# Second feed-forward block: its up product as seven half-size products per pair of weight blocks

## The chip, the cores and the metric

One core of a Trainium2 chip runs the program. The metric is the device time of one execution in microseconds (us). Engines are written as the profile writes them: PE is TensorE (matmuls; PEld its weight loads), ACT is ScalarE, DVE is VectorE, POOL is GpSimd, SP is SyncE, which issues the DMAs of the weights.

## The reference

A block of a network on 512 tokens (plus 256 context tokens) of width 1024: a feed-forward sublayer, a mixer (delta rule and attention), and a second feed-forward sublayer. The last one is what the change touches, on the 512 tokens alone:

```python
def _ffn_sublayer(x, shift, scale, gate, pre_g, post_g, w_gu, w_down):
    h = _modulate(_rmsnorm(x, pre_g), shift, scale)
    a, b = jnp.split(h @ w_gu, 2, axis=-1)
    y = (jax.nn.silu(a) * b) @ w_down
    return x + FFN_RES_WEIGHT * gate * _rmsnorm(y, post_g)
```

`w_gu` is 1024 x 5632 and `w_down` 2816 x 1024, in float32. All is computed to nearly float32 accuracy.

## The kernel before

Activations lie with the features on the 128 partitions: h is 8 tiles of 128 features by 512 tokens. A float32 product is made of three passes: each operand is split in a rounded part (`_hi`) and the rest (`_lo`), and `hi*hi + lo*hi + hi*lo` is accumulated in PSUM. A weight block is 128 outputs by 1024 inputs (8 slices of 128, 512 KB). Its way is the same everywhere: SP loads it to one of four slots of `raw` (`load`: it waits until `w_split` says that the slot's old block has been split); ACT rounds it to `w_hi` (`split`, L776); DVE subtracts to make `w_lo` (L1475) and raises `w_split`; PE uses it (`gemm`, L2283).

The second feed-forward block has 22 pairs of up blocks: one block of a pair is for `a` (its 128 columns), the other for `b`. ACT reads `a` out of PSUM through silu (`sg`), DVE multiplies with `b` (`gt`), ACT rounds (`g2_hi`), DVE subtracts (`g2_lo`). The 22 pairs are cut in chunks of 8, 8 and 6, and after each chunk comes a down product of 8 blocks (16 half blocks after the last: `last_down`), so that only 8 hidden tiles are held. Here a block is 8 slices x 3 passes = 24 matmuls of 512 columns.

The first two pairs are special (`first_up`): their matmuls are 256 columns wide, since the tokens' second half is still being normalised (`h_tile` on ACT, `n_scale` and `h_low` on DVE) when PE starts on the first.

The first feed-forward block of the same kernel already runs 20 of its 22 pairs in another way, as seven products of half size (a Winograd form of Strassen's scheme). A pair of blocks and the tokens are seen as a 2 x 2 matrix each: the weights' quarters are 4 slices of one block, the tokens' quarters 4 slices by half the tokens. Seven products of such quarters or of sums of them (A11, A12, S2, S3, S1, A22, S4) give the four quarters of the result where the plain way takes eight. POOL makes the four sums of weights of a pair (`weight_sums`, L641 to L648), ACT and DVE split all seven, two places of PSUM are added up by ACT and DVE. There a product is 12 matmuls of 384 columns.

Order of work is written out by hand on every engine; engines are in-order and wait on semaphores (`u_hi` and `u_lo`: how many quarters are rounded and split; `u_mm`: how many products are done; `w_loaded0..3`: a slot of `raw` is loaded; `w_split`: blocks split; `s_add`: weight sums made).

Of the kernel before, what the change touches and what calls it, by code (L numbers as in the profile page):

```python
# [23 lines left out]
P = 128  # L24
# [99 lines left out]
SLOTS = product_slot(N_SEVEN - 1, S4) + 1  # L124

# [52 lines left out]
def build(nc, W, WMOD, XT, VEC, CONV, CA, CB, OUT, XS, GR):  # L178
    ctx = ExitStack()
    with ctx:  # L180
# [140 lines left out]
        f_lo = at("f_lo", 148, [KT, SEQ], F32R)  # L321
        z_t = at("z_t", 87.5, [4, HALF])
# [146 lines left out]

        def token_sum(i):  # L470
# [295 lines left out]


        @block.scalar
        def _(a):
# [173 lines left out]
            def h_tile(h, k):  # L943
                n = KT * h + k
                a.wait_ge(s("nrm_ready"), 4 * KT + n + 1)
                if n >= 4:
                    a.wait_ge(s("h_ready"), 4 * KT + n - 3)
                a.activation(z_u[:, k % 4], z_t[:, k % 4], ACT.Identity, bias=mod[:, 48 + k, 1:2], scale=drv[:, 4, k, 1:2])\
                 .then_inc(s("h_full"), 1)
                a.wait_ge(s("h_full"), 4 * KT + n + 1)  # L950
                a.activation(f_hi[:, k, xhalf(h)], z_u[:, k % 4], ACT.Copy).then_inc(s("h_rounded"), 1)
# [125 lines left out]
            def ffn(i, b0, seg_list):  # L1077
                lo = seg_list[0][0]
                for kind, b, n, c, hid in ffn_parts(b0):
                    if kind == "down" and c == 2:  # L1080
# [3 lines left out]

                    def up(it):
                        first = i and c == 0 and isinstance(it, int)
                        for j in range(4):
                            blk = Blk(b, it, j)
                            if not first:
                                step(blk)  # L1090
                            elif j < 2:
                                a.wait_ge(s("gemm_done"), blk.n + 1)
                                split(blk.ahead(4))
                            if first and j == 2:
                                a.wait_ge(s("gemm_done"), blk.n + 1)
                                a.activation(sg[:, CTX:T], first_bank(blk, j), ACT.Silu).then_inc(psum_read[blk.pair], 1)
                            elif j % 2 == 0:
                                read_out(blk, lambda l, h_: sg[:, l:h_], seg_list, ACT.Silu)
                            else:

                                a.wait_ge(psum_read[blk.pair], blk.turn + 2)
                                p_ = it * 2 + j // 2
                                a.activation(cols(g_hi, g2_hi, i, bass.ds(p_, 1), lo, T), gt[:, lo:T], ACT.Copy).then_inc(s("g_rounded"), 1)

                    def down(it):
                        for j in range(4):
                            blk = Blk(b, it, j)
                            step(blk)
                            if c == 0:
                                read_out(blk, lambda l, h_: cols(Y, Y2, i, bass.ds(it * 4 + j, 1), l, h_), seg_list)  # L1110
                    if i and kind == "up" and c == 0:
                        up(0)
                        with a.Fori(1, n // 4, 1) as it:
                            up(it)
                    else:
                        loop(a, n // 4, up if kind == "up" else down)
# [343 lines left out]
            for k in range(KT):  # L1460
                x_square(1, k)
            x_rstd(1)
            for k in range(KT):
                h_tile(1, k)
            a.preload_act_table_set(SILU_SET)
            ffn(1, B_FFN2, segs_x)
# [3 lines left out]
        def _(v):  # L1470
# [145 lines left out]
            def h_low(h, k):  # L1616
# [5 lines left out]
                v.tensor_tensor(f_lo[:, k, xhalf(h)], z_u[:, k % 4], f_hi[:, k, xhalf(h)].bitcast(F32), ALU.subtract).then_inc(s("h_ready"), 1)  # L1622
# [135 lines left out]
            def ffn(i, b0, seg_list):  # L1758
                lo = seg_list[0][0]
                pairs = i * HID  # L1760
                for kind, b, n, c, hid in ffn_parts(b0):
                    if kind == "down" and c == 2:
                        all_read(v, b - 2 * FCH[c])
# [1252 lines left out]
```

## Time and profile before

| | |
|---|---|
| median of 3 runs | 1921.43 us (1920.65 to 1922.58) |
| the profiled execution | 1924.11 us, its span 1922.4 us |
| granted TensorE clock, mean | 0.996 |
| PE busy | 1873.6 us, 97% of the span |
| DVE busy | 1167.9 us, 61% |
| ACT busy | 893.4 us, 46% |
| POOL busy | 412.7 us, 21% |
| last part of the program | from 1569 us on: second feed-forward block past its first two pairs |

The span is the time from the first to the last instruction; the execution's own time is 1.7 us longer. The 40 slices of the page show the granted clock at nine tenths or more in each. In the last third of the span POOL has nothing to do.

### The profile page before, as it was taken

The page shows a single profiled execution, that of the slowest core. Times are in us where ns is not written, and L with a number is a line of the kernel's source. Part 1 is how long each engine was busy: PE and PEld are TensorE (multiplying, and loading weights), DVE is VectorE, ACT ScalarE, POOL GpSimd, SP SyncE. Part 2 cuts the span into 40 slices and gives each one's busy share as a digit, 9 for nine tenths or more (in the row PEclk, how much of TensorE's full clock was granted, in tenths as well). Part 3 has the DMA queues.
Part 4 walks back from the last instruction along what each step waited for, and adds up shares of the span by engine and source line. Part 5 has one row for each costly group of instructions (what it writes and reads, how often), then busy time and mean ns, then how long its engine had stood idle before and what let it go on. Part 6 is the DMA issues. An engine that isn't in the chain of part 4 may idle for free.

```text
span 1922.4 us, 30414 instructions
## 1 busy us (share of the span) xinstructions
PE 1873.6 (97%) x11233; PEld 1720.1 (89%) x11233; DVE 1167.9 (61%) x1918; ACT 893.4 (46%) x1637; POOL 412.7 (21%) x314
## 2 busy tenths in 40 slices
PE   8899999999998999999999999999999999999997
PEld 5899999999997799999999999987888888888887
DVE  6758787878666765567766776676333543233336
ACT  6534242424457655557655665564223542222223
POOL 0713141323100200256345634540000000000000
PEclk9999999999999999999999999999999999999999
DMA  8233435553423410011111111112334313333332
GB/s 325 67 121 123 130 110 164 175 189 117 143 77 113 124 53 1 27 35 61 49 40 36 55 49 49 33 33 66 98 98 141 100 45 91 96 97 99 99 98 77
DMA packets 52221, 178.09 MB, mean 93 GB/s; under 512 B 6820, under 2 KB 10020, under 8 KB 51888
## 3 DMA queue, kind: packets, MB, share of 16 engines
q1 hardware_dynamic: 48864, 162.46, 26.0%
q0 software_dynamic: 3280, 14.60, 2.4%
q8 instruction: 48, 0.79, 0.2%
q14 instruction: 29, 0.24, 0.0%
HBM read 170.17 MB, written 4.24 MB: 91 GB/s over the span
## 4 chain that ended last, share of the span: by engine, by line
PE 84%; DVE 6%; ACT 5%; issue 2%; POOL 1%; DMA 1%; SPq 0%; ACTq 0%; DVEq 0%
PE ps L2283 61%; PE ps L2482 14%; PE ps L2287 4%; PE ps L2764 1%; PE ps L2688 1%; DMA raw<-W 1%; DVE d_os L2183 1%; DVE d_c L2051 1%; PE ps L2718 1%; PE ps L2820 1%; ACT w_hi L776 1%; ACT L1294 0%; DVE w_lo L1475 0%; DVE m_prod L1837 0%; ACT c_u L875 0%
## 5 line engine op out<-in xcount | busy, mean ns | idle before, releaser
L1475 DVE TENSOR_TENSOR w_lo<-raw,w_hi 128x1024 fp32r<-128x1024 f32 (+1 forms) x137 | 167.9, 1226 | 233.8 <-ACT w_hi L776 233.8
L776 ACT ACTIVATE w_hi<-raw 128x1024 fp32r<-128x1024 f32 x137 | 144.7, 1056 | 340.8 <-PE ps L2283 338.8
L2283 PE MATMUL ps<-h_hi,w_hi 128*128 128x512 f32 (+2 forms) x736 | 245.2, 372 | 9.4 <-DVE h_lo L1545 3.0
L2283 PE MATMUL ps<-h_lo,w_hi 128*128 128x512 f32 (+2 forms) x736 | 241.0, 360 | 0.0
L2283 PE MATMUL ps<-h_hi,w_lo 128*128 128x512 f32 (+2 forms) x736 | 232.1, 356 | 0.0
L2283 PEld LDWEIGHTS ps<-h_hi,w_hi 128*128 128x128 f32 x736 | 132.8, 188 | 29.9 <-DVE h_lo L1545 6.7
L2283 PEld LDWEIGHTS ps<-h_hi,w_lo 128*128 128x128 f32 x736 | 135.9, 188 | 13.5
L2283 PEld LDWEIGHTS ps<-h_lo,w_hi 128*128 128x128 f32 x736 | 136.0, 188 | 12.9 <-issue 1.2
L2283 PE MATMUL ps<-f_hi,w_hi 128*128 128x512 f32 (+1 forms) x352 | 135.0, 384 | 3.2 <-ACT Y L1417 1.9
L2283 PE MATMUL ps<-g_hi,w_hi 128*128 128x384 f32 (+2 forms) x444 | 132.9, 346 | 1.7 <-DVE g_lo L1793 1.0
L2283 PE MATMUL ps<-f_hi,w_lo 128*128 128x512 f32 (+1 forms) x352 | 133.9, 380 | 0.0
L2283 PE MATMUL ps<-f_lo,w_hi 128*128 128x512 f32 (+1 forms) x352 | 133.9, 380 | 0.0
L2283 PE MATMUL ps<-g_lo,w_hi 128*128 128x384 f32 (+2 forms) x444 | 131.7, 343 | 0.0
L2283 PE MATMUL ps<-g_hi,w_lo 128*128 128x384 f32 (+2 forms) x444 | 131.7, 343 | 0.0
L2105 DVE TENSOR_TENSOR d_w<-ps,cb 128x512 f32<-128x512 f32 x120 | 83.0, 692 | 55.5 <-PE ps L2287 52.5
L2482 PE MATMUL ps<-h_lo,w_hi 128*128 128x384 f32 x320 | 107.6, 336 | 2.2 <-ACT pb L1030 2.2
L708 POOL TENSOR_TENSOR d_s<-d_l,cb 128x256 f32<-128x256 f32 (+1 forms) x80 | 91.4, 1162 | 77.4 <-DVE d_kd L2088 73.1
L2482 PE MATMUL ps<-h_hi,w_hi 128*128 128x384 f32 x320 | 107.7, 337 | 0.2 <-DVE ps L1694 0.2
L2482 PE MATMUL ps<-h_hi,w_lo 128*128 128x384 f32 x320 | 107.3, 335 | 0.0
L2482 PE MATMUL ps<-x_lo,w_hi 128*128 128x384 f32 x320 | 107.1, 335 | 0.0
L1343 ACT ACTIVATE d_qu<-ps 128x512 f32<-128x512 f32 (+1 forms) x144 | 80.8, 561 | 45.6 <-PE ps L2764 40.7
L2283 PEld LDWEIGHTS ps<-g_hi,w_hi 128*128 128x128 f32 x444 | 81.5, 188 | 8.7 <-DVE g_lo L1793 1.2
(391 smaller groups left out, 4635.3 us busy)
## 6 DMA issues: line engine op xcount, KB each, us to landing
raw<-W SPq DMA_DIRECT2D x221, 512.0 KB, 3.6
w_mod<-WMOD SPq DMA_DIRECT2D x68, 512.0 KB, 3.7
g_row<-g_rows POOLq DMA_DIRECT2D x8, 768.0 KB, 4.5
X<-XT SPq DMA_DIRECT2D x4, 768.0 KB, 7.9
a_sw<-i_n POOLq DMA_DIRECT2D x40, 64.0 KB, 1.9
w_first<-WMOD SPq DMA_DIRECT2D x4, 512.0 KB, 11.9
X<-XT SPq DMA_DIRECT2D x1, 2048.0 KB, 14.0
x_spill<-X POOLq DMA_DIRECT2D x1, 2048.0 KB, 8.4
```

The costliest lines, as they stand in the source:

```text
L708: g.tensor_tensor(d_s[lv % 2][:, c0:c1], d_l[:, 0, c0:c1], off_mask[:, lv, :].unsqueeze(1).to_broadcast([P, c1 - c0, P]), ALU.mult).then_i ...
L776: a.activation(hi, src, ACT.Copy).then_inc(s("w_hi"), 1)
L1343: a.activation(d_qu[:, i % 2, 0:m].rearrange("p c n -> p (c n)"), solver_out(i), ACT.Copy)\
L1475: v.tensor_tensor(lo, src, hi.bitcast(F32), ALU.subtract).then_inc(s("w_split"), 1)
L2051: v.scalar_tensor_tensor(c, d_up[:, lo + i:lo + i + n], tap, c, ALU.mult, ALU.add)\
L2105: v.tensor_tensor(d_w[:, gr].rearrange("p (m c) n -> p m c n", m=2), ps[:, TRB[gr], 0:2 * P].rearrange("p (c n) -> p c n", c=2).unsqueeze( ...
L2183: v.scalar_tensor_tensor(d_os[:], d_q2[:], EPS * DH * DH, d_os[:], ALU.mult, ALU.add).then_inc(s("od_add"), 1)
L2283: return pe.matmul(out, lhsT, rhs, start=start, stop=stop)
L2287: return pe.matmul(out, lhsT, rhs, start=False, stop=True, skip_group_check=True)
L2482: last = pe.matmul(out_, slot_of((w_hi, w_hi, w_lo)[i], n + pos, k), (hi, lo, hi)[i][pos][:, k], start=pos in (A11, A12, S3) and k == 0 an ...
L2688: last = pe.transpose(ps[:, c // 3, P * (c % 3):P * (c % 3) + P], a_p[:, i % 2, P * c:P * c + P], ident)
L2718: last = pe.transpose(ps[:, ((2, 7), (0, 1))[i][c // 3], P * (c % 3):P * (c % 3) + P], d_c[:, 1 + i, off[c]:off[c] + P], ident)
```

## The change

`first_up` keeps the first two pairs. The other 20 pairs, in chunks of 6, 8 and 6, are made of seven products each, with half of the tokens (256 columns) and half of the block's slices: 12 matmuls of 256 columns a product. The order of a chunk's products interleaves a pair with the next (`order2`). The split quarters go to a ring of twelve slots, and ACT and DVE run eight products ahead of PE (`AHEAD2`). The plain quarters (A11, A12, A22) are also copied by ACT from `raw` into PSUM banks 5 to 7, and DVE takes them from there when it subtracts; the four sums stay in SBUF. `w_split` is raised by two when S4 of a pair, the last quarter that needs `raw`, is split. The tokens' sums are made by POOL and DVE during and after the normalisation. Down products stay as they are; `last_down` takes its first two blocks slice by slice in turn. The diff, cut to its core:

```diff
+def order2(c):
+    pairs, out = CH2[c], [(CH2[c][0], A11), (CH2[c][0], A12)]
+    for q in pairs:
+        more = q != pairs[-1]
+        out += [(q, S2), (q, S3)] + [(q + 1, A11)] * more + [(q, S1), (q, A22)] + [(q + 1, A12)] * more + [(q, S4)]
+    return out
...
+            def weight_sums2(q):
...
+                g.tensor_tensor(s3, a1, b1, ALU.subtract).then_inc(s("s_add"), 1)
+                if q == 1:
+                    g.wait_ge(s("g_ready"), HID + N_CONV + 1)
+                if q >= 2:
+                    g.wait_ge(s("u_lo"), SLOTS + AT2[q - 2, S1] + 1)
+                g.tensor_tensor(s1, b1, b2, ALU.add).then_inc(s("s_add"), 1)
...
+                g.tensor_tensor(s2, s1, a1, ALU.subtract).then_inc(s("s_add"), 1)
+                if q:
+                    g.wait_ge(s("u_lo"), SLOTS + AT2[q - 1, S4] + 1)
+                g.wait_ge(s("s_add"), done + 3)
+                g.tensor_tensor(s4, a2, s2, ALU.subtract).then_inc(s("s_add"), 1)
...
+            def copy_weights(q, pos):
+                blk = pair_blocks(q)[int(pos == A22)]
+                a.wait_ge(w_loaded[blk.raw], (blk.load + 1) * 16)
...
+                a.activation(copy_bank(pos), weight_part2(q, pos), ACT.Copy)
+            def round_weights(q, pos):
...
+                if n >= RING2:
+                    a.wait_ge(s("u_mm"), SLOTS + AT2[q, pos] - RING2 + 1)
...
+                a.activation(slot2(True, q, pos), weight_part2(q, pos), ACT.Copy).then_inc(s("u_hi"), 1)
...
+                for c in range(3):
+                    order, pairs = ORDER2[c], CH2[c]
+                    for i, (q, pos) in enumerate(order):
+                        after_product2(q, pos)
+                        lo, hi = (first_copies(i - 1), first_copies(i)) if c == 0 else (i + AHEAD2, i + AHEAD2 + 1)
+                        for p in order[lo:hi]:
+                            weights_hi(*p)
...
+            def weights_lo(q, pos):
...
+                src = copy_bank(pos) if pos in (A11, A12, A22) else weight_part2(q, pos)
+                v.wait_ge(s("u_hi"), SLOTS + AT2[q, pos] + 1)
+                v.tensor_tensor(slot2(False, q, pos), src, slot2(True, q, pos).bitcast(F32), ALU.subtract).then_inc(s("u_lo"), 1)
+                if pos == S4:
+                    v.wait_ge(s("u_lo"), SLOTS + AT2[q, pos] + 1)
+                    v.sem_inc(s("w_split"), 2)
...
+            def product2(q, pos):
...
+                pe.wait_ge(s("u_lo"), SLOTS + AT2[q, pos] + 1)
...
+                if pos in (S2, S1, A22):
+                    pe.wait_ge(s("p_copy"), 3 * done + (S2, S1, A22).index(pos) + 1)
+                if pos == S4:
+                    pe.wait_ge(s("p_sum"), 3 * done + 2)
...
+                for k in range(4):
+                    for i in range(3):
+                        last = pe.matmul(out_, w[i][:, k], (hi, lo, hi)[i][:, k], start=pos in (A11, A12, S3) and k == 0 and i == 0,
+                                         stop=True, skip_group_check=True)
+                last.then_inc(s("u_mm"), 1)
...
             def last_down():
-                for n in range(2 * KT):
...
+                first = [Blk(B_LAST, 0, n) for n in range(2)]
+                for k0, k1 in ((0, 5), (5, 6)):
```

ACT in the up product of the second chunk onwards, before: two blocks of one pair. `w_hi<-raw` is the rounding of the block two ahead, `sg` the silu, `g_hi<-gt` the rounded gate.

```order
L776 ACTIVATE w_hi<-raw 128x1024 [waits w_loaded1,gemm_done]
L786 ACTIVATE sg<-ps 128x512
L780 REGISTER_ALU
L776 ACTIVATE w_hi<-raw 128x1024 [waits w_loaded2,gemm_done]
L1101 REGISTER_ALU
L1103 ISA [waits psum_read0]
L1103 ACTIVATE g_hi<-gt 128x512
```

ACT now, in the steady part, from the place after product S3 of a pair q to the place after A12 of pair q+1. `f_pb` and `f_pa` are results taken out of PSUM; `ps<-raw` is the copy of a plain quarter and the row behind it its rounding: A11 of pair q+2, then (after `f_s1a`, the sum S1 of q+1) A22 of q+1, then A12 of q+2; `f_s_201` is S4 of q+1.

```order
L1290 ACTIVATE f_pb<-ps 128x256 [waits u_mm]
L1226 ACTIVATE ps<-raw 128x512 [waits u_lo,w_loaded3]
L1242 ACTIVATE w_hi<-raw 128x512 [waits u_mm]
L1283 ACTIVATE f_pa_203<-ps 128x256 [waits p_gate,u_mm]
L1242 ACTIVATE w_hi<-f_s1a 128x512 [waits s_add,u_mm]
L1226 ACTIVATE ps<-raw 128x512 [waits u_lo,w_loaded2]
L1242 ACTIVATE w_hi<-raw 128x512 [waits u_mm]
L1226 ACTIVATE ps<-raw 128x512 [waits u_lo,w_loaded3]
L1242 ACTIVATE w_hi<-raw 128x512 [waits u_mm]
L1293 ACTIVATE f_pa_203<-f_pa_203 128x256 [waits p_sum]
L1242 ACTIVATE e_hi<-f_s_201 128x512 [waits s_add,u_mm]
```

So two roundings of a pair became seven, with three copies and five readings between them, and the rounding of S4 stands nine rows behind the copy of the next-but-one pair's first quarter. DVE at the same place, now (its first row splits A11 of q+2, `f_s1a` is S1 of q+1, L2050 and L2053 add up results of pair q, L2033 is the gate, L2045 the sum that ACT's silu waits for, `f_s_201` is S4 of q+1):

```order
L1992 TENSOR_TENSOR w_lo<-ps,w_hi 128x512 [waits u_hi]
L1992 TENSOR_TENSOR w_lo<-f_s1a,w_hi 128x512 [waits u_hi]
L2050 TENSOR_TENSOR ps<-ps,f_pb 128x256 [waits g_ready,p_copy,u_mm]
L1992 TENSOR_TENSOR w_lo<-ps,w_hi 128x512 [waits u_hi]
L2053 TENSOR_TENSOR ps<-ps,f_pb 128x256 [waits u_mm]
L1992 TENSOR_TENSOR w_lo<-ps,w_hi 128x512 [waits u_hi]
L2033 TENSOR_TENSOR ps<-f_pa_204,ps 128x256 [waits p_sum,p_silu]
L2045 TENSOR_TENSOR f_pa_203<-ps,f_pa_203 128x256 [waits p_copy,u_mm]
L1992 TENSOR_TENSOR e_lo<-f_s_201,e_hi 128x512 [waits u_hi]
```

Before, DVE had four instructions for a whole pair (two L1475 of 1024, `gt`, `g_lo`). Behind the last row it raises `w_split`, for which SP waits with the next load. POOL, which had nothing here before, now has for each pair:

```order
L877 TENSOR_TENSOR f_s_200<-raw 128x512 [waits u_lo,w_loaded2,w_loaded1]
L882 TENSOR_TENSOR f_s1a<-raw 128x512 [waits u_lo]
L888 TENSOR_TENSOR f_s_199<-f_s1a,raw 128x512 [waits s_add,u_lo]
L892 TENSOR_TENSOR f_s_201<-raw,f_s_199 128x512 [waits s_add,u_lo]
```

These are S3, S1, S2 and S4, in that order; the first waits for both blocks of the pair, the last for the split of the S4 before it.

## Rows read from the trace of the kernel before

**Rows 1.** The page: busy time of PE; the chain that ended last, by line.
```profile
PE 1873.6 (97%) x11233; PEld 1720.1 (89%) x11233; DVE 1167.9 (61%) x1918; ACT 893.4 (46%) x1637; POOL 412.7 (21%) x314
...
PE ps L2283 61%; PE ps L2482 14%; PE ps L2287 4%; PE ps L2764 1%; PE ps L2688 1%; DMA raw<-W 1%; DVE d_os L2183 1%; DVE d_c L2051 1%; PE ps L2718 1%; PE ps L2820 1%; ACT w_hi L776 1%; ACT L1294 0%; DVE w_lo L1475 0%; DVE m_prod L1837 0%; ACT c_u L875 0%
```

**Rows 2.** Windows: busy us of each engine in one window, clock, DMA share, GB/s.
```profile
1680.00:1740.00 60.00, 60.00 (x267) 49.69 (x266) 20.10 (x22) 17.36 (x23) 0.00 (x0) 1.00 0.30 96
```

**Rows 3.** Timeline of PE: start us, us, engine, line, operation, tiles, shapes, [idle before].
```profile
1569.38 0.50 PE L2283 MATMUL ps<-f_hi,w_hi 128*128 128x512 f32 x1 [0.92 <-ACT sg L1096]
...
1579.72 0.39 PE L2283 MATMUL ps<-f_hi,w_hi 128*128 128x512 f32 x1
...
1592.41 0.39 PE L2283 MATMUL ps<-f_hi,w_lo 128*128 128x512 f32 x1
...
1879.80 0.28 PE L2283 MATMUL ps<-g_lo,r_hi 128*128 128x256 f32 x1
...
1884.00 0.28 PE L2283 MATMUL ps<-g_hi,r_hi 128*128 128x256 f32 x1
```

**Rows 4.** Groups of PE from 1400 us on: count, busy us, mean ns, idle before.
```profile
L2283 PE MATMUL ps<-g_hi,w_hi 128*128 128x256 f32 x24 | 7.1, 294 | 1.0 <-DVE g_lo L1793 1.0
```

**Rows 5.** Timeline of ACT.
```profile
1500.29 0.38 ACT L918 ACTIVATE sqb<-ps 128x256 f32<-128x256 f32 x1 [1.27 <-PE ps L2283]
1500.57 0.38 ACT L1417 ACTIVATE Y<-ps 128x256 f32<-128x256 f32 x1
...
1556.03 0.42 ACT L951 ACTIVATE f_hi<-z_u 128x256 fp32r<-128x256 f32 x1
...
1556.97 0.42 ACT L951 ACTIVATE f_hi<-z_u 128x256 fp32r<-128x256 f32 x1
...
1562.12 1.28 ACT L1465 ACT_TABLE_LOAD   x1
...
1568.22 0.63 ACT L1103 ACTIVATE g_hi<-gt 128x512 fp32r<-128x512 f32 x1 [0.46 <-DVE gt L1782]
1568.75 0.58 ACT L1096 ACTIVATE sg<-ps 128x512 f32<-128x512 f32 x1
```

**Rows 6.** Timeline of DVE.
```profile
260.20 1.70 DVE L1654 TENSOR_TENSOR w_lo<-raw,w_hi 128x512 fp32r<-128x512 f32 x1
261.83 0.68 DVE L1654 TENSOR_TENSOR w_lo<-sums,w_hi 128x512 fp32r<-128x512 f32 x1
262.43 0.68 DVE L1654 TENSOR_TENSOR w_lo<-raw,w_hi 128x512 fp32r<-128x512 f32 x1
...
1543.71 0.42 DVE L1596 TENSOR_TENSOR z_y<-Y,z_ys 128x256 f32<-128x256 f32 x1
1544.05 0.48 DVE L1605 SCALAR_TENSOR_TENSOR X<-z_y,drv,X 128x256 f32<-128x256 f32 x1
...
1603.54 1.23 DVE L1475 TENSOR_TENSOR w_lo<-raw,w_hi 128x1024 fp32r<-128x1024 f32 x1 [0.30 <-ACT w_hi L776]
```

**Rows 7.** Timeline of POOL at the same place as the first of rows 6.
```profile
260.06 1.29 POOL L644 TENSOR_TENSOR sums<-raw 128x512 f32<-128x512 f32 x1
```

**Rows 8.** Groups by shape of DVE and POOL over the whole span.
```profile
L1489 DVE SCALAR_TENSOR_TENSOR m_prod<-w_mod,ps 128x1024 bf16<-128x1024 f32 x56 | 68.1, 1216 | 2.1
L1654 DVE TENSOR_TENSOR w_lo<-sums,w_hi 128x512 fp32r<-128x512 f32 x80 | 59.9, 753 | 34.9 <-ACT w_hi L990 34.1
...
L1489 DVE SCALAR_TENSOR_TENSOR m_prod<-w_mod,sil_row 128x1024 bf16<-128x1024 f32 x24 | 36.5, 1519 | 0.4
...
L708 POOL TENSOR_TENSOR d_s<-d_l,cb 128x256 f32<-128x256 f32 x48 | 33.4, 723 | 73.1 <-DVE d_kd L2088 73.1
```

**Rows 9.** SP: an issue in this stage; landing of a pair's first load; of both.
```profile
1604.94 0.33 SPq L527 DMA_DIRECT2D raw<-W  x1
...
DMA to landing us min/median/max: 3.6/3.6/3.6
...
DMA to landing us min/median/max: 3.6/4.1/4.5
```

More of the change, by code:

```diff
@@ L768, in _ @@
+            g.wait_ge(s("t_lo"), 6)
+            for q in range(1, N_SEVEN):
+                weight_sums2(q)
         @block.scalar
@@ new lines, in weights_hi, with token_hi2 @@
+            def weights_hi(q, pos):
+                if pos in (A11, A12, A22):
+                    copy_weights(q, pos)
+                round_weights(q, pos)
+            def token_hi2(i):
+                if i == 0:
+                    a.wait_ge(s("t_add"), 24)
+                if i in (1, 3):
+                    a.wait_ge(s("t_lo"), (0, 5, 0, 6)[i])
+                if i == 2:
+                    a.wait_ge(s("t_add"), 28)
+                    a.wait_ge(s("d_mm"), 17)
+                x, hi, lo = token_sum2(i)
+                a.activation(hi, x, ACT.Copy).then_inc(s("t_hi"), 1)
@@ L1083, in ffn @@
                         return
[L1085 to L1116, printed above, removed]
+                    for j in range(KT):
+                        blk = down2(c, j)
+                        a.wait_ge(s("gemm_done"), blk.n + 1)
+                        if c == 0:
+                            a.activation(Y2[:, j], bank(blk, 1), ACT.Copy).then_inc(psum_read[blk.pair], 1)
+                        if j + 2 < KT:
+                            split(down2(c, j + 2))
+                        for p in ORDER2[c + 1][2 * j - 8:2 * j - 6] if j >= 4 else ():
+                            weights_hi(*p)
             a.preload_act_table_set(SILU_SET)
@@ L1461, in _ @@
                 x_square(1, k)
+                if k in (1, 5):
+                    copy_weights(0, (A11, A12)[k // 4])
+                if k in (3, 7):
+                    round_weights(0, (A11, A12)[k // 4])
             x_rstd(1)
@@ L1464, in _ @@
                 h_tile(1, k)
[L1465 to L1466 removed]
+            ffn2()
         @block.vector
@@ L1756, in ffn1 @@
                 ffn1_last()
[L1758 to L1763, printed above, removed]
+            def weights_lo(q, pos):
+                if chunk2(q) == 0 and AT2[q, pos] in (0, 2):
+                    v.wait_ge(s("h_ready"), 5 * KT if AT2[q, pos] == 0 else 6 * KT)
+                src = copy_bank(pos) if pos in (A11, A12, A22) else weight_part2(q, pos)
[4 more added lines that the diff above has]
+                    v.sem_inc(s("w_split"), 2)
@@ L1806, in ffn @@
-                    if kind == "down" and c:
-                        all_read(v, b - 2 * FCH[c])
-                    if i and kind == "up" and c == 0:
-                        up(0)
-                        with v.Fori(1, n // 4, 1) as it:
-                            up(it)
-                    else:
-                        loop(v, n // 4, up if kind == "up" else down, c == 2)
+                    for j in range(KT):
+                        blk = down2(c, j)
+                        if c:
+                            v.wait_ge(s("gemm_done"), blk.n + 1)
+                            v.tensor_tensor(Y2[:, j], Y2[:, j], bank(blk, 1), ALU.add).then_inc(psum_read[blk.pair], 1)
+                        if j + 2 < KT:
+                            split(down2(c, j + 2))
+                        for p in ORDER2[c + 1][2 * j - 8:2 * j - 6] if j >= 4 else ():
+                            weights_lo(*p)
@@ L2550, in ffn @@
-                    if kind == "up" and c == 0:
-                        body(0)
-                        with pe.Fori(1, n // 4, 1) as it:
-                            body(it)
-                    else:
-                        loop(pe, n // 4, body)
+                    for j in range(KT):
+                        gemm(down2(c, j), g2_hi, g2_lo, segs_x, FCH[c], off=CTX,
+                             ready=(s("g_ready"), HID + sum(FCH[:c]) + 1) if j == 0 else None)
             pe.wait_ge(s("sil_rows"), 1)
```

386 lines of the change are left out of this document (311 added, 75 removed).

## The prediction

> **What bounds the kernel now.** I read the page first: PE is busy for 97% of the span, and the chain that ended last runs through its matmuls [rows 1]. A window of 60 us in the stage that changes shows PE busy for all of it at full clock, DVE and ACT for a third, POOL not at all [rows 2]. So the time of this stage is the number of matmuls times their step, and anything else costs only where PE comes to wait for it. Last come the timelines for steps, from start to start, since records of one engine overlap: a matmul of 512 columns takes 12.69 us over 56 steps, 0.2266 us; one of 256 columns 4.20 over 35, 0.120 us, more than half [rows 3]. That is the price of the narrower product.
>
> **The change, part by part.** *Matmuls.* A pair was 48 matmuls of 512 columns, 10.88 us; it becomes 84 of 256, 10.08 us. Twenty pairs give 15.9 us. Two idle places go too: 0.92 us before the first block behind `first_up`, which waited for the silu of the block just before it (A11 needs an older bank) [rows 3], and 1.0 us before the last hidden tile of `last_down`, now asked for later [rows 4]. Together 17.8 us. Down products are the same.
>
> *The load on the helpers.* An ACT instruction that follows another directly starts 0.53 us after it for 512 columns, 0.28 us for 256 out of PSUM, 0.1 less than it lasts [rows 5]. For a pair ACT has eleven of 512 and five of 256 columns, about 7.3 us. DVE's steps are 0.60 us for 512 and 0.34 for 256 [rows 6]; it has eight and five, 6.5 us. POOL has four sums of 1.29 us [rows 7]. All are under 10.08, so none is the bound by its load.
>
> *The round trip of a load.* This is new, and I take it for the bound. `raw` holds four blocks, two pairs. The loads of pair q+3 wait for the split of S4 of pair q+1, and the first thing ACT does with a block is the copy of A11, an in-order instruction: behind the copy of A11 of q+2 stand in ACT's row all that lead to S4 of q+1. So once per pair: block landed, ACT, DVE, ACT, DVE, SP, DMA, next block landed. Let the first block of q+2 land at 0. ACT does copy and rounding of A11 (1.06), the reading of `f_pa` (to 1.34), the rounding of S1 (to 1.97), then starts four more, the last at 3.46, ready at 4.09. DVE splits A12 from 4.1, gates from 4.7, adds for `f_pa` from 5.04 to 5.46. ACT's silu is at 5.5, its rounding of S4 starts 0.32 later (256 columns from SBUF last 0.42 [rows 5], less the 0.1) and ends at 6.45; DVE splits S4 by 7.2. SP's issue comes 0.17 us behind the end of such a split (1603.54 and 1.23, to 1604.94) [rows 6, 9], and a pair's first load lands after 3.6 us [rows 9]: 11.0 us. PE would like 10.08.
>
> To that comes a hold on DVE. The trace shows a split of 512 columns with both operands in SBUF that took 1.70 us instead of 0.68; it began 0.14 us after a POOL sum of 1.29 us, and ended 0.55 us behind it [rows 6, 7]. A DVE operation with one operand in PSUM keeps its 1216 ns in the mean, its twin with both in SBUF has 1519 [rows 8]; so the copies to PSUM shield three of seven splits. The second block of a pair lands 4.5 us after an issue 0.47 later, so 1.4 us behind the first [rows 9], and POOL starts S3 of q+2 then, to 2.7. The split of S1 of q+1 is due at 2.0, in that sum: it runs from 2.7 to 3.4. DVE is then in a row: add S1 (3.3 to 3.75), A22 (3.64), add (4.24), A12 (4.58), gate (5.18), add for `f_pa` (5.52 to 5.94). Silu, rounding of S4 to 6.93, split to 7.66, SP and DMA: 11.4 us. I take 11.4; the free 11.0 and a second hold (12) are the bounds. The mean of all such splits with sums, 753 ns, speaks for the free value [rows 8], but there POOL was idle for most of a 14.5 us pair.
>
> The Trainium skill (SBUF — State Buffer, "SBUF: two separate sides") calls this an exclusive lock, held for the whole instruction, in which the loser fully blocks, also for a DVE operation with two SBUF inputs against a GpSimd operation that reads SBUF. By that rule every collision costs the rest of the sum, and the trip is the 11.4 us; by the mean row it would be 11.0.
>
> *What the trip costs.* PE feels it at S4 of pair q, which waits for the add of S1, 3.8 us after the landing for q+2. Chunks two and three: at the first product's start ACT has four copies and roundings left (2.1 us), then `f_pa`, S4 to 3.0, DVE to 3.8; the first load lands at 7.5. S4 of the chunk's pair k would start undisturbed at 11.5 + 10.08k, and starts at 7.5 + 11.4k + 3.8 if that is later, up to the last pair that has a pair two behind it. In the chunk of eight that is k = 5: 68.3 against 61.9, 6.4 us late. In the chunk of six k = 3: 45.5 against 41.8, 3.7 us late. Up to k = 0 the ring hides it. PE doesn't get this back.
>
> *The first chunk* starts with the tokens' sums to make. From the end of the normalisation, 1562.1 [rows 5], ACT has four instructions of 1024 columns (two steps of 512 each), 14 of 512, three of 256 and the table load of 1.28 us up to the rounding of the first S4, 13.8 us; DVE has as much. Following both rows wait by wait I get 17.3 us until S4 is split. And the normalisation is longer: per tile of 0.94 us on ACT [rows 5] DVE has two operations of two SBUF operands with little room, while POOL runs its weight sums and eight token sums of 0.72 us [rows 8]; I take 2.5 us, between 0 and 5. So the first load lands at 1562.1 + 17.3 + 2.5 + 3.8 = 1585.7. PE ends `first_up` at 1568.5 [rows 3]: 17.2 us after that, not 7.5. With k = 3 (the first trip lacks `f_pa`, 11.1): 17.2 + 33.9 + 3.8 = 54.9 against 41.8, 13.1 us late.
>
> *Sum.* 17.8 less 13.1, 6.4 and 3.7 is 5.4 us lost. The profiled execution took 1924.1 us (span 1922.4), 2.7 over the median; put on the median of 1921.4 the forecast is 1926.8, rounded 1927 us.
>
> The ends: a trip of 11.0 and an add at 3.3 make 11.2, 3.9 and 2.1 us late at the same start, 0.6 us gained; with the normalisation undisturbed as well, 3 us gained. A trip of 10.6 (a shorter gap at every hand-over) and that start give about 10.6 us late, 1914. A trip of 12 makes 15 + 9.5 + 5.6, 12 us lost, 1934.
>
> **Rivals.** *The ring hides the trip* (faster). If ACT's row slips behind the loads only once, eight products of lead (11.5 us) absorb it, and PE waits only in the first chunk, for the token sums, some 3 us: 1921.4 - 17.8 + 3 = 1907. For it: the low loads of ACT and DVE, and that the same scheme in the first feed-forward block leaves PE busy. Against: there loads start at A22's split, a pair has 14.5 us, and the trip is per pair, so lead is used up and not refilled. It decides at a trip of 10.1 us. *The trip without hold*, 11.0 us: 1920 to 1921, no change. *A longer trip*: two holds per pair, or loads that land at 4.5 instead of 3.6 us, or PE's stalls of 1.3 us per pair lowering its clock (no row shows what such stalls do): 1934 or more. *The change doesn't do what it says*: a product of 256 columns with operands out of the ring could step slower than 0.120 us; each 0.001 us more costs 1.7 us. Rows at that width with split operands read from three places show 0.120, so I give it little.
>
> **How the numbers follow.** Forecast (11.4) 45%; no hold (11.0) 20%; hidden 20%; longer 15%. A change of 0.2% (3.8 us: 1917.6 to 1925.3) is about what a measurement of this kernel can tell. Forecast falls to slower in 40 of 45 and to no change in 5; no hold to no change in 12, faster in 8; hidden is faster; longer is slower. Faster 0.28, same 0.17, slower 0.55. For 8 in 10 the range reaches from 1909 to 1936; the likeliest case's own is 1921 to 1932.
>
> **What would show it.** Steps of 0.120 us in the products. PE idle before S4's matmuls, put down to DVE's add at L2050, about 1.3 us for most pairs and more in the first chunk; the issues of SP's pair loads 11.4 us apart in the second chunk; ACT idle before its copy at L1226 of A11, put down to the DMA. DVE's splits from sums well over 0.69 us, those from PSUM at 0.69. The stage of the third chunk (six pairs) in some 64 us. It is wrong if the pair loads come 10.1 us apart, if ACT never waits for `raw`, or if the first chunk's products start on time.

## The result, and the profile after

The changed kernel took 1932.9 us in the median of 4 runs (1931.97 to 1934.18), the kernel before 1921.05 us beside it; the ratio is 1.0061, 95% interval 1.0043 to 1.0078. So it is slower, by about 12 us, where the forecast had 5.4 us; it was 1927 us, with a range from 1909 to 1936. The profiled execution took 1934.18 us (span 1932.5), that of before 1924.11 (span 1922.4): 10.1 us are there to be explained by these two traces.

The page of the changed kernel, busy time and the start of the chain's lines (against [rows 1]: 720 matmuls more, PE busy for 11 us less, and loads of `raw` at 3% of the chain in place of 1%):

```profile
PE 1863.0 (96%) x11953; PEld 1743.4 (90%) x11953; DVE 1273.3 (66%) x2108; ACT 982.3 (51%) x1881; POOL 535.2 (28%) x402
...
PE ps L2579 49%; PE ps L2792 14%; PE ps L2583 4%; DMA raw<-W 3%; PE ps L2879 2%; PE ps L3103 1%; PE ps L3027 1%; ACT e_hi L1242 1%; DVE e_lo L1992 1%; DVE d_os L2476 1%; DVE d_c L2344 1%; PE ps L3057 1%; PE ps L3159 1%; ACT w_hi L1242 1%; ACT w_hi L917 1%
```

Windows by stage (length, busy us of each engine with its instructions, PE's clock, DMA). First the kernel before, from its first block behind `first_up` to `last_down`, and `last_down` to the end:

```profile
1569.38:1874.16 304.78, 304.78 (x1344) 252.45 (x1345) 98.31 (x104) 83.18 (x103) 0.00 (x0) 1.00 0.32 98
1874.16:1922.40 48.24, 36.95 (x297) 35.98 (x295) 31.13 (x72) 15.85 (x29) 0.00 (x0) 0.93 0.25 77
```

Then the changed kernel: up and down products of chunk one, of chunk two, the up products of chunk three, and the rest:

```profile
1569.39:1643.05 73.66, 63.75 (x506) 62.46 (x505) 54.90 (x82) 45.10 (x95) 27.44 (x20) 0.98 0.30 101
1643.05:1686.60 43.55, 43.55 (x194) 36.04 (x193) 14.10 (x14) 15.54 (x24) 9.52 (x7) 1.00 0.23 73
1686.60:1775.16 88.56, 82.61 (x673) 81.12 (x672) 63.27 (x98) 56.09 (x120) 35.71 (x26) 1.00 0.31 108
1775.16:1818.71 43.55, 43.55 (x194) 36.05 (x193) 18.13 (x21) 12.15 (x17) 10.30 (x7) 1.00 0.23 73
1818.71:1884.12 65.41, 61.57 (x505) 60.78 (x504) 46.30 (x73) 40.37 (x87) 23.71 (x18) 1.00 0.34 113
1884.12:1932.50 48.38, 36.96 (x298) 35.99 (x296) 29.91 (x71) 15.26 (x29) 0.00 (x0) 0.91 0.20 66
```

The difference of the two spans stands here whole. At 0.120 us a matmul the chunks need 60.5, 80.6 and 60.5 us (504, 672, 504 matmuls); they take 73.7, 88.6 and 65.4, so they are 13.2, 7.9 and 4.9 us late, 26.0 together. The 960 matmuls of 512 columns of before took 304.78 less twice 43.55, 217.7 us; 201.6 + 26.0 is 227.6. That is the stage's 9.95 us; `last_down` and what follows give 0.14 more, what lies before the first product 0.01. I call these 26.0 us the lateness, and the experiments are read by it too.

The 0.01 hides two things of opposite sign. The same matmul of `first_up`, in the kernel before and in the changed one:

```profile
1538.61 0.35 PE L2283 MATMUL ps<-f_hi,w_hi 128*128 128x256 f32 x1 [1.88 <-ACT Y L1417]
1537.16 0.36 PE L2579 MATMUL ps<-f_hi,w_hi 128*128 128x256 f32 x1 [1.88 <-ACT Y L1642]
```

This execution was 1.45 us ahead there, and has lost that again by the first product (30.77 us from here to it before, 32.23 now). From this matmul to the end the changed kernel takes 11.55 us more, near the 11.85 us between the medians.

Some of what PE and ACT waited for from 1569 to 1884 us (total, times, longest):

```profile
ACT ps L1226 <- DMA raw<-W: 14.9, 14, 4.0
PE ps L2879 <- DVE ps L2050: 14.0, 11, 3.7
PE ps L2879 <- ACT f_pb L1286: 2.3, 3, 1.7
PE ps L2879 <- DVE e_lo L1992: 1.7, 1, 1.7
PE ps L2879 <- ACT f_pb L1290: 1.4, 3, 0.6
```

One round of the second chunk, on PE, SP, ACT, DVE and POOL (start, length, engine, line, operation):

```profile
1732.63 0.36 PE L2879 MATMUL ps<-f_hi,e_hi 128*128 128x256 f32 x1 [1.33 <-DVE ps L2050]
1743.99 0.35 PE L2879 MATMUL ps<-f_hi,e_hi 128*128 128x256 f32 x1 [1.06 <-DVE ps L2050]
...
1724.95 1.20 SPq L623 DMA_DIRECT2D raw<-W  x2
...
1736.60 0.92 SPq L623 DMA_DIRECT2D raw<-W  x2
...
1728.38 0.60 ACT L1226 ACTIVATE ps<-raw 128x512 f32<-128x512 f32 x1 [0.49 <-DMA raw<-W]
...
1734.70 0.42 ACT L1293 ACTIVATE f_pa<-f_pa 128x256 f32<-128x256 f32 x1 [2.31 <-DVE f_pa L2045]
1735.03 0.61 ACT L1242 ACTIVATE e_hi<-f_s 128x512 fp32r<-128x512 f32 x1
...
1740.33 0.60 ACT L1226 ACTIVATE ps<-raw 128x512 f32<-128x512 f32 x1 [0.79 <-DMA raw<-W]
...
1730.35 1.79 DVE L1992 TENSOR_TENSOR w_lo<-f_s1a,w_hi 128x512 fp32r<-128x512 f32 x1
1732.07 0.42 DVE L2050 TENSOR_TENSOR ps<-ps,f_pb 128x256 f32<-128x256 f32 x1
...
1735.67 0.69 DVE L1992 TENSOR_TENSOR e_lo<-f_s,e_hi 128x512 fp32r<-128x512 f32 x1 [1.01 <-ACT e_hi L1242]
...
1730.32 1.28 POOL L877 TENSOR_TENSOR f_s<-raw 128x512 f32<-128x512 f32 x1 [4.22 <-DVE w_lo L1992]
```

The block lands at 1728.38. DVE's split of S1 meets POOL's sum and takes 1.79 us; the add behind it ends at 1732.49, and PE starts S4 at 1732.63. DVE's row is late by as much, the silu starts at 1734.70, S4 is rounded at 1735.03 and split at 1735.67, SP issues at 1736.60, the next block lands at 1740.33: a trip of 11.95 us. The others in this chunk took 11.36, 10.99, 11.04 and 11.12 us (ACT's waits at 1694.99, 1706.35, 1717.34, 1728.38, 1740.33, 1751.45).

Note that the idle of a row understates how late PE is. It counts from the modelled end of the matmul before, 0.28 us after its start, where an undisturbed step is 0.12: a wait listed as 1.33 puts PE 1.49 us back.

### The profile page after: what moved, and what is told of

It is laid out like the page before. It is cut to its first block, busy times and chain, and to the rows that moved or that the text cites. A ratio compares the mean times of both kernels' runs of the same rounds, so it can differ in the third digit from the quotient of the medians.

```text
span 1932.5 us, 32403 instructions
## 1 busy us (share of the span) xinstructions
PE 1863.0 (96%) x11953; PEld 1743.4 (90%) x11953; DVE 1273.3 (66%) x2108; ACT 982.3 (51%) x1881; POOL 535.2 (28%) x402
## 4 chain that ended last, share of the span: by engine, by line
PE 73%; DVE 9%; ACT 8%; issue 4%; DMA 3%; POOL 1%; SPq 0%; ACTq 0%; DVEq 0%; POOLq 0%
PE ps L2579 49%; PE ps L2792 14%; PE ps L2583 4%; DMA raw<-W 3%; PE ps L2879 2%; PE ps L3103 1%; PE ps L3027 1%; ACT e_hi L1242 1%; DVE e_lo L1992 1%; DVE d_os L2476 1%; DVE d_c L2344 1%; PE ps L3057 1%; PE ps L3159 1%; ACT w_hi L1242 1%; ACT w_hi L917 1%
## 5 line engine op out<-in xcount | busy, mean ns | idle before, releaser
L1703 DVE TENSOR_TENSOR w_lo<-raw,w_hi 128x1024 fp32r<-128x1024 f32 (+1 forms) x97 | 121.1, 1248 | 120.8 <-ACT w_hi L917 120.8
L917 ACT ACTIVATE w_hi<-raw 128x1024 fp32r<-128x1024 f32 (+1 forms) x97 | 101.8, 1049 | 142.7 <-PE ps L2579 140.8
L2879 PE MATMUL ps<-f_hi,e_hi 128*128 128x256 f32 x344 | 98.5, 286 | 13.5 <-DVE ps L2050 9.2
L737 POOL TENSOR_TENSOR sums<-raw 128x512 f32<-128x512 f32 x20 | 28.8, 1442 | 277.9 <-DVE w_lo L1882 177.8
L2879 PE MATMUL ps<-f_hi,e_lo 128*128 128x256 f32 x344 | 97.2, 283 | 0.0
L877 POOL TENSOR_TENSOR f_s<-raw 128x512 f32<-128x512 f32 x20 | 29.3, 1466 | 228.4 <-DMA raw<-W 151.0
## 6 DMA issues: line engine op xcount, KB each, us to landing
w_first<-WMOD SPq DMA_DIRECT2D x4, 512.0 KB, 11.4
X<-XT SPq DMA_DIRECT2D x1, 2048.0 KB, 13.1
```

The source lines that it names most:

```text
L737: g.tensor_tensor(s1[:], b1, b2, ALU.add).then_inc(s("s_add"), 1)
L877: g.tensor_tensor(s3, a1, b1, ALU.subtract).then_inc(s("s_add"), 1)
L917: a.activation(hi, src, ACT.Copy).then_inc(s("w_hi"), 1)
L1703: v.tensor_tensor(lo, src, hi.bitcast(F32), ALU.subtract).then_inc(s("w_split"), 1)
L2879: last = pe.matmul(out_, w[i][:, k], (hi, lo, hi)[i][:, k], start=pos in (A11, A12, S3) and k == 0 and i == 0, stop=True, skip_group_check ...
```

## The experiments

For each, the lateness of the chunks is the length of its three windows less 60.5, 80.6 and 60.5 us, read from the one execution that was profiled. Times given with a run are medians, and all ratios are to the kernel before.

| kernel | lateness by chunk, us | sum | ratio, 95% interval |
| --- | --- | --- | --- |
| changed kernel | 13.2, 7.9, 4.9 | 26.0 | 1.0061, 1.0043 to 1.0078 |
| e1_release | 9.5, 3.3, 0.8 | 13.6 | 0.9992, 0.9983 to 1.0001 |
| e2_small_sums | 12.7, 6.2, 2.5 | 21.5 | 1.0032, 1.0023 to 1.0041 |
| e3_no_copies | 17.8, 13.0, 5.9 | 36.7 | 1.0121, 1.0106 to 1.0137 |
| e4_copy_twice | 16.4, 12.4, 6.8 | 35.5 | 1.0118, 1.0103 to 1.0134 |
| e5_gate_first | 5.2, 0.5, 0.0 | 5.7 | 0.9959, 0.9946 to 0.9973 |
| e6_release_small_sums | 5.8, 0.8, 0.0 | 6.6 | 0.9963, 0.9950 to 0.9976 |
| e7_first_order | 3.7, 0.5, 0.0 | 4.2 | 0.9949, 0.9936 to 0.9963 |
| e8_gate_first_copy_twice | 6.1, 0.6, 0.2 | 6.9 | 0.9966, 0.9953 to 0.9979 |
| e9_last_block | 3.3, 0.5, 0.0 | 3.8 | 0.9952, 0.9939 to 0.9966 |

### Give the blocks back earlier

`raw` of a pair is last read for A22's rounding and POOL's S4 sum; the split of S4 reads only a sum.

```diff
             def weights_lo(q, pos):
...
-                if pos == S4:
+                if pos == A22:
+                    v.wait_ge(s("s_add"), 4 * (N_SEVEN + q) + 4)
                     v.wait_ge(s("u_lo"), SLOTS + AT2[q, pos] + 1)
                     v.sem_inc(s("w_split"), 2)
```

> Edit: the two blocks of a pair are given back for loading when A22 of the pair is split (and POOL's sum for S4 is made), not when S4 is split. Nothing else changes. Theory (the round trip of a load is the bound): the chain from landing to landing gets shorter by the stretch from A22's split to S4's split, to some 7.5 us, under the 10.08 us that PE wants; ACT waits no more for a load before its copy of A11 in the second and third chunk, PE's idle before S4 goes, and of the 26 us by which the three chunks are late (13.2, 7.9, 4.9) some 8 to 9 stay: the token sums in the first chunk and about 1.2 us in the last pair of each chunk. 1932.9 - 17.5 = 1915 to 1916 us. Rival (the ring hides the load and the hand-overs of ACT, DVE and PE are themselves the bound): PE's idle before S4 stays at about 1 us a pair, 1928 to 1933 us.

1921.28 us. The theory holds in kind: in the second and third chunk ACT waits no more for a load, and the lateness falls from 26.0 to 13.6 us (by 3.7, 4.6 and 4.1 us in the three chunks). But I expected 8 to 9, and a time of 1915 to 1916. Against the kernel before this is no clear difference. What is left in the middle of the chunks is a second chain: S4 of pairs 1 to 4 and 10 to 12 still starts 0.3 to 0.7 us late, the pairs 10.5 to 10.6 us apart. Its place, on DVE and POOL:

```profile
1738.20 1.82 DVE L1992 TENSOR_TENSOR w_lo<-f_s,w_hi 128x512 fp32r<-128x512 f32 x1
1739.95 0.42 DVE L2034 TENSOR_TENSOR ps<-f_px,ps 128x256 f32<-128x256 f32 x1
...
1738.18 1.29 POOL L892 TENSOR_TENSOR f_s<-raw,f_s 128x512 f32<-128x512 f32 x1 [3.40 <-DVE e_lo L1992]
...
1740.40 0.60 ACT L1274 ACTIVATE g_hi<-ps 128x512 fp32r<-128x512 f32 x1 [1.43 <-DVE ps L2034]
```

The split of S4 releases POOL's next S4 sum, and DVE's next operation, the split of S2, runs into it. The gate (L2034) stands behind that split, ACT's rounding of the gate waits for it by 1.43 us, and the copies and roundings of the next pair stand behind that.

### Take POOL's sums out of DVE's way

```diff
-                g.tensor_tensor(s3, a1, b1, ALU.subtract).then_inc(s("s_add"), 1)
+                n_ = P if q < 2 else 16
+                g.tensor_tensor(s3[:, :, 0:n_], a1[:, :, 0:n_], b1[:, :, 0:n_], ALU.subtract).then_inc(s("s_add"), 1)
```

(and the other three alike)

> Edit: from the third pair on POOL sums only 16 of 128 columns of each tile, so its four sums per pair keep their order and waits but are short; what ACT and DVE then split of the rest is an older sum (this part of the computation is left out). Theory (trip of 11.0 us plus holds of DVE by POOL's sums): the trips of the changed kernel, 11.36, 10.99, 11.04, 11.95, 11.12 in the second chunk and 11.22, 12.90, 11.10 in the third, all become 11.0; PE gets back 1.5 and 2.2 us, and up to 0.5 in the first chunk: 1929 us; the splits from sums all last 0.69 us. Rival (holds are most of the loss): 1915 to 1920 us, trips near 10.1. Rival (holds cost nothing since other waits swallow them): 1932 to 1933 us.

1927.5 us, 4.5 us less lateness: by this, holds are about a sixth of the 26 us, the trip itself the larger part. The trips went to 10.83, 11.04, 10.84, 11.44 and 12.10 us in the second chunk; so not all became 11.0. The last one, on SP and ACT:

```profile
1745.66 1.20 SPq L623 DMA_DIRECT2D raw<-W  x2
...
1750.44 0.60 ACT L1227 ACTIVATE ps<-raw 128x512 f32<-128x512 f32 x1 [2.81 <-DMA raw<-W]
```

It took 4.8 us from issue to landing. Of the 14 loads in this trace that ACT waited for, five took 4.1 to 4.8 us; in the changed kernel one of 14 did, 4.75 us in its longest trip (1845.63 to 1850.38, 12.90 us, third chunk), where its others have 3.4 to 3.9. Those late loads put back part of what the missing holds gave, so the sixth is rather a lower bound. What makes a load late I didn't settle.

### Read the loaded blocks directly

```diff
             def copy_weights(q, pos):
...
-                a.activation(copy_bank(pos), weight_part2(q, pos), ACT.Copy)
...
             def weights_lo(q, pos):
...
-                src = copy_bank(pos) if pos in (A11, A12, A22) else weight_part2(q, pos)
+                src = weight_part2(q, pos)
```

> Edit: ACT doesn't copy the three plain quarters to PSUM; DVE reads them from the loaded block in SBUF. Without holds the trip would lose ACT's copies of A11, A22 and A12, 1.57 us, but DVE's row becomes its own chain: about 10.4 us, PE gets back most of its waits, 1922 us. Theory (DVE's operations with both operands in SBUF wait for the end of a POOL sum that they meet): the splits of A22 and A12 now meet POOL's sums S1 and S2 as well, two more holds of 0.5 to 0.9 us in DVE's row: trip about 12.2 us, 0.9 more than now, times 5, 3 and 3 trips that PE feels, some 10 us: 1943 us. The splits of A22 and A12 would show means well over 0.69 us.

1945.8 us, 10.7 us more lateness, as the theory of holds had it; the trips of the second chunk took 12.5 us in the mean (11.6 to 13.7) where 12.2 was expected. Not all of it is the trip: in most pairs PE now loses 0.6 to 0.8 us each before A11 and A22, put to ACT's readings of results, and a load that took 4.98 us was followed by a stall of 2.99 us. The same 39 splits of plain quarters as groups (count, busy us, mean ns), in the changed kernel and then in this one:

```profile
L1992 DVE TENSOR_TENSOR e_lo<-ps,e_hi 128x512 fp32r<-128x512 f32 x39 | 26.5, 683 | 21.9 <-ACT e_hi L1242 21.9
```

```profile
L1991 DVE TENSOR_TENSOR e_lo<-raw,e_hi 128x512 fp32r<-128x512 f32 x39 | 46.9, 1210 | 15.7 <-ACT e_hi L1241 15.4
```

With one operand in PSUM 683 ns in the mean, with both in SBUF 1210. The copies cost ACT twenty times 1.57 us, and they are worth it. By the Trainium skill (SBUF — State Buffer, "SBUF: two separate sides") a DVE operation with two SBUF inputs and a GpSimd operation that reads SBUF exclude each other for the whole instruction. The trace agrees: the split at 1730.35, which began 0.03 us after the start of a sum of 1.28, ended at 1732.14, 0.54 us behind the sum's end.

### Lengthen the trip on purpose

```diff
             def copy_weights(q, pos):
...
+                if pos == A11:
+                    a.activation(copy_bank(pos), weight_part2(q, pos), ACT.Copy).then_inc(s("conv_loaded"), 1)
+                    a.wait_ge(s("conv_loaded"), 16 + q + 1)
                 a.activation(copy_bank(pos), weight_part2(q, pos), ACT.Copy)
```

> Edit: ACT makes the copy of A11 twice, one after the other with a wait between, 0.55 to 0.65 us more right behind the landing; the values stay the same. Theory (round trip of a load): every trip is 0.6 us longer, and PE feels 3 + 5 + 3 of them: 6 to 7 us slower, 1939 to 1940 us; the issues of SP's pair loads in the second chunk come 11.9 us apart in place of 11.3. Rival (PE is bound by something else, and ACT, busy for 7.3 of 10 us, has room): within 1 us of 1933 us.

1944.8 us, 9.5 us more lateness, well past 1 us, and past my 6 to 7 as well. The trips are 11.4 to 12.6 us. One part of the surplus is the clock (0.94 in the second chunk, 1.00 in the changed kernel). Windows from the start of an S4 that came 2.82 us late, and of the same length right behind it:

```profile
1750.46:1756.36 5.90, 5.89 (x27) 5.90 (x28) 4.74 (x8) 2.17 (x6) 1.92 (x2) 0.50 0.15 47
1756.64:1762.54 5.90, 5.90 (x52) 5.90 (x51) 3.96 (x6) 5.54 (x12) 2.69 (x2) 1.00 0.32 119
```

After an idle of 2.82 us PE ran at half its clock, 1.2 GHz, for 5.9 us: 27 steps of 0.213 us where 0.120 is usual, some 2.5 us lost. A stall of 1.82 us at 1725.37 was followed by 3.2 us at half clock, 1.56 us lost. But what PE loses so is lateness only if PE wouldn't have waited anyway. The next S4 behind either, on PE, and the add on DVE that the second needs:

```profile
1737.34 0.35 PE L2882 MATMUL ps<-f_hi,e_hi 128*128 128x256 f32 x1 [0.18 <-DVE ps L2053]
1763.24 0.28 PE L2882 MATMUL ps<-f_hi,e_hi 128*128 128x256 f32 x1
...
1761.62 0.42 DVE L2053 TENSOR_TENSOR ps<-ps,f_pb 128x256 f32<-128x256 f32 x1
```

The first still waited for DVE, so by the rows those 1.56 us cost next to nothing; at the second the add was done at 1762.04, so at most 1.1 us are the clock's. The rest, some 8.4 us, is more than the 6 to 7 expected. The sum of the expectation left something out: the doubled copy stands also between the last landing of a chunk and the add behind it. And the mean trip of the second chunk rose by 0.7 us (11.3 to 12.0), not 0.6. How the rest divides isn't shown.

### Early release and the gate ahead of the held split

On top of the early release:

```diff
             def after_product2(q, pos):
...
+                if pos == S4 and q != CH2[chunk2(q)][-1]:
+                    gate2(q, 1)
                 if q != CH2[chunk2(q)][0]:
-                    if pos == S2:
-                        gate2(q - 1, 1)
```

> Edit: the early release of e1_release, and DVE makes the second half of a pair's gate (L2034, from f_px) right after the silu, ahead of the split of the next pair's S2 and not behind it. Theory (in e1_release pairs run 10.5 to 10.6 us apart because POOL's sum for S4 holds the split of S2 for 1.1 us, the gate behind it comes late, ACT rounds the gate late, then copies and rounds late, and PE waits at S4): with the gate ahead of the held split this chain is 1.4 us shorter, PE no longer waits at S4 in the middle of a chunk, the 0.35 us of each pair go (about 5 in the first chunk, 3 in the second, 1 in the third), 3 us less than e1_release's 1921.3: 1918 us. Rival (the 0.35 us come from somewhere else, for example from the adds of DVE or ACT's own row): 1921 us, same idle places.

1914.6 us, 3.4 under the expectation, and the first kernel that clearly beats the one before. The windows of its three chunks:

```profile
1570.18:1635.83 65.65, 62.48 (x507) 62.13 (x505) 53.62 (x81) 44.43 (x94) 27.67 (x19) 0.97 0.34 113
1679.38:1760.49 81.11, 80.85 (x673) 80.68 (x672) 62.55 (x98) 57.25 (x120) 34.97 (x26) 1.00 0.34 118
1804.04:1864.53 60.49, 60.49 (x506) 60.48 (x504) 45.95 (x73) 41.32 (x87) 23.63 (x18) 1.00 0.37 123
```

Chunks two and three run at PE's pace to 0.5 us. With the gate, the waits in the last pair of a chunk went too (0.8 us at A22): there the reading of S3's bank stood in ACT's row behind the rounding of the gate. The holds are still there (splits of sums 0.94 to 1.38 us in the mean of a group); in these two chunks they cost nothing now.

The cross-check, with the gate where it was and POOL's sums short:

> Edit: the early release of e1_release together with POOL's short sums of e2_small_sums (16 of 128 columns of the sums from the third pair on; this part of the computation is left out). Theory: with the round trip off the path, holds of DVE by POOL are what is left inside the chunks: the 0.35 us per pair go as with the moved gate, 1917.5 to 1919 us; against e1_release 2.5 to 4 us. If holds alone (not the trip) were the cause of most of the loss, this would also be the first kernel near 1910 us.

1915.3 us, 2.2 under the expectation: the other way to remove the same chain gives nearly the same time. Short sums gave 4.5 us of lateness with the trip on the path and 7.0 with it off.

The same copy made twice, on this base:

> Edit: e5_gate_first, and ACT makes the copy of A11 twice, as in e4_copy_twice. Theory: the same 0.6 us that cost 10 us there (it was in the round trip that sets the pace) costs little where the trip has slack: at most 1 to 2 us over e5_gate_first, 1918 to 1920 us. Rival (ACT's load as such is what PE waits for): again 9 to 11 us, 1928 us or more.

1916.2 us, 1.7 more than e5_gate_first and 1.2 us more lateness, most of it at the start, against 9.5 us in the changed kernel. So ACT's load as such isn't what PE waited for, its place in the trip was.

### The first chunk

This one starts from e5_gate_first. In the changed kernel PE's S2 of the first pair starts 1.9 us late. The timeline of PE and then ACT:

```profile
1574.14 0.36 PE L2879 MATMUL ps<-f_hi,e_hi 128*128 128x256 f32 x1 [1.72 <-DVE e_lo L1992]
...
1573.63 0.37 ACT L1283 ACTIVATE f_pa<-ps 128x256 f32<-128x256 f32 x1
```

The row names DVE's `e_lo`, but S2 also needs the bank that ACT empties into `f_pa`, done at 1574.00.

```diff
             def ffn2():
...
                 token_hi2(3)
+                after_product2(0, A11)
                 weights_hi(*ORDER2[0][4])
...
-                        after_product2(q, pos)
+                        if q or pos not in (A11, A12):
+                            after_product2(q, pos)
+                        if (q, pos) == (0, S2):
+                            after_product2(0, A12)
```

> Edit: e5_gate_first, and in ACT's row for the first pair only: the reading of A11's bank into f_pa comes ahead of the copy of the next A11 and two roundings, and the silu of A12 comes behind the reading of S2's bank. Theory (the first chunk's loss that isn't the round trip is ACT's in-order row, in which PE's S2 waits 1.9 us for the reading of A11's bank and S1 0.7 us for that of S2's behind a silu that waits for DVE): the first chunk comes 2 to 2.5 us earlier than in e5_gate_first, 1915.5 to 1916 us. Rival (DVE's row, full without a gap from the tokens' sums to the third product, sets the start): the idle before S2 moves to S3 or S1 and nothing is won, 1918 us.

1912.45 us, the fastest, 2.1 us under e5_gate_first, near the 2 to 2.5 expected, but not for the reason expected. The wait at S2 is gone, so the name in that row was wrong, and the first chunk is 1.5 us shorter. But the waits only moved: S1 now waits 0.50, A22 1.32 (put to DVE) and S4 0.80 us, 2.6 us for the three, where e5_gate_first had 1.23 at S2 and 1.94 at S1. DVE is busy for 14.50 of this chunk's first 14.85 us, so the rival is right on the waits. The 1.5 us are the clock. Windows of the first 20 us of the chunk, and of 3.2 us behind the stall of 1.94 us, in e5_gate_first:

```profile
1570.18:1590.00 19.82, 16.65 (x125) 16.30 (x124) 17.54 (x23) 12.87 (x27) 9.73 (x6) 0.91 0.20 64
1582.00:1585.20 3.20, 3.20 (x18) 3.20 (x17) 3.20 (x4) 3.20 (x8) 1.67 (x1) 0.50 0.26 105
```

and of the first 20 us in e7_first_order:

```profile
1570.15:1590.00 19.85, 17.04 (x137) 16.32 (x136) 18.35 (x25) 14.63 (x31) 9.86 (x7) 1.00 0.27 89
```

Fifteen steps of 0.213 us in place of 0.120 are 1.4 us. About the same waits in smaller pieces left the clock at full, and here PE meets no later wait that would have hidden the loss.

### The last down product

This one starts from e7_first_order. The forecast booked a gain of 1.0 us here; the changed kernel has 1.03 us of idle at 1889.63, put to DVE's `r_lo`, where before had 0.96 for `g_lo` [rows 4].

```diff
             def last_down():
...
+                split(blks[2])
                 for i, blk in enumerate(blks):
...
-                    if i + 2 < KT:
+                    if 0 < i < KT - 2:
                         split(blks[i + 2])
```

and on ACT `a.preload_act_table_set(LOG_SET)` moves ahead of `gate_round2(pairs[-1])`.

> Edit: e7_first_order, and behind the last pair DVE splits the third block of the last down product ahead of its first addition to Y2 and not behind it, and ACT loads its table ahead of the last rounding of a gate and not behind it. Theory (the 1.0 us of idle at the last down product, which the forecast counted as won, only moved from the gate's low part to the split of the third block, which stands behind ACT's table load of 1.28 us and DVE's addition that waits for PE): r_lo is ready by about 4.2 us after that product's start and PE wants it at 4.3, so the 1.03 us go: 1911.4 us, 0.05% less than e7_first_order. Rival (the gate's low part gets late again, since its rounding starts 0.8 us later): the idle stands before the last hidden tile of the first two blocks, nothing is won, 1912.5 us.

The idle became 0.57 us, put to DVE's addition to `Y2`, which must empty the bank; from the last product to the end 47.9 us in place of 48.4 in e7_first_order. The times don't tell the two apart (1913.2 and 1912.45 us). About half of the idle stayed, moved once more.

## Why the prediction was right, and where it was off

The number lies in the stated range but above the 1921 to 1932 us of the likeliest case; the loss was about twice the forecast. The mechanism was the one forecast, and what was missing are terms of the sum.

**Step of a product:** 0.120 us, as taken; no 256-column product is slower except behind long stalls. The gain of 15.9 us is there (217.7 - 201.6 = 16.1).

**The round trip:** right in mechanism, and near in size. Landing to landing 11.0 to 11.95 us in the second chunk, mean 11.3, forecast 11.4, bounds 11.0 and 12; the first landing at 1586.3 was forecast for 1585.7. S4 of pair 3 of the first chunk was forecast for 54.9 us behind 1568.5, that is 1623.4, and started at 1622.80; S4 of the sixth pair of the second chunk for 1686.6 + 68.3 = 1754.9, and started at 1755.13; that of the third chunk's fourth pair for 1864.2, and started at 1864.63. That these three come within 0.6 us is partly luck, since errors cancel: the first load of the second chunk landed 8.4 us after the first product, not 7.5, and its trips were 0.1 us shorter each; in the third chunk the mean trip was 11.7 us, with the late load in it, and the add followed the last landing sooner. The early release shows the trip as a cause (12.4 of 26.0 us of lateness gone), the doubled copy on both bases confirms it. Most of the first chunk's 13.2 us is not its work: with the release early 9.5 stay.

**The hold:** the forecast had one size of it, the trace has three. In the 11 trips the split of S1 lasted 0.69 us twice, 1.03 to 1.21 seven times and 1.72 or 1.79 twice. In the second chunk the trip without hold took 10.99, that with 1.79 us 11.95, the others 11.04 to 11.36. The mean of 11.3 is between the forecast's two cases, and short sums bring the shortest trips of that chunk to 10.83, near the 11.0 of the free value. The longest trip of all, 12.90 us, has both a long hold and a late load.

**Sum.** The lateness was forecast as 23.2 us and is 26.0. At the last S4 that feels the trip it was 11.7, 6.6 and 4.2 us against 13.1, 6.4 and 3.7. The term that was missing is what comes behind it: 1.5, 1.3 and 0.8 us up to the end of each chunk, nearly all in the last pair, where PE waits for ACT's readings into `f_pb`, which I hadn't worked out at all. The clock isn't such a term, though in the first chunk the idle of 3.69 us before 1588.68 was followed by 3.2 us at half clock (window of the changed kernel):

```profile
1589.61:1592.81 3.20, 3.20 (x17) 3.20 (x16) 2.20 (x6) 1.57 (x5) 2.29 (x2) 0.50 0.00 0
```

PE lost 1.6 us in it, but S4 of pair 2, at 1611.98, waited another 1.40 us for the add behind the trip: without the loss it would have waited that much longer.

**The two small gains** of 0.92 and 1.0 us were booked and didn't come. The first idle is gone, but the product starts at 1569.39, 0.01 us later than before: the normalisation holds PE up by 1.68 and 0.41 us at 1556.11 and 1558.71 (DVE's `f_lo`, beside POOL's sums). Since this execution was 1.45 us ahead at 1537, these waits cost 2.4 us and not 0.9. I had charged that slip, put at 2.5 us, to the loads only, not to `first_up`. That POOL's sums make it is argued from the rows; no run moved them. The second gain moved to the next split, as above. Together 2.1 us, with 2.8 more of lateness, less 0.2 of further gain in the steps, 4.7 of the 10.1 us; the forecast's own 5.4 are the rest.

**Rivals.** "The ring hides the trip" is out: with the trip off the path the kernel is at once 10 us and more faster. "A longer trip" named stalls that lower the clock: those of 1.3 us that it spoke of didn't, the one of 3.69 us at the start did, and by the rows cost next to nothing beyond the trip. Loads that land late, which it named too, came once.

## What to carry to other kernels

When a load's buffer is given back by a signal that stands at the end of a chain of helper engines, add up landing to landing before adding up any engine's load: helpers that are busy for 71, 63 and 40% of a chunk (DVE, ACT and POOL in the second) can be slower than the engine they feed. Then ask what reads the buffer last; moving one signal from the split of S4 to that of A22 was worth 12 us, about as much as the change had lost. Once a cycle is off the path, the next one may stand right behind it: measure again before the next saving is booked, and look behind each removed wait for what stands next in its engine's row.

## What the runs showed that I had not expected

- Stalls of PE of 1.82, 1.94, 2.82 and 3.69 us were followed by 3.2 us (behind that of 2.82, 5.9 us) at half its clock, 1.2 in place of 2.4 GHz, in which PE loses another 1.5 to 2.5 us; whether the kernel loses them depends on whether PE would have waited at its next stop anyway. But one of 2.05 us in the changed kernel (S4 at 1854.03), one of 1.81 (S4 at 1753.60 with the short sums) and one of 1.58 (at 1713.25 with the copy doubled) were followed by steps at full clock. What decides between them stays open.
- Holds go both ways: POOL's S1 sums, 1.29 us alone, took 1.60 and 1.86 us in the mean of the two groups of the changed kernel.
- Loads of one kind, issued alone, mostly land 3.4 to 3.9 us after their issue, and others at 4.1 to 5.0; what delays them stays open.
